# Eight stick-breaking heads, their filler slots in two orders, in a two-layer decoder trunk on one core

## What is computed

```python
def stick_breaking(q, k, v):                      # 8 heads
    z = einsum('bqhd,bkhd->bhqk', q_blk, k) * scale
    log_1m = where(causal, log_sigmoid(-z), 0.0)
    suffix = cumsum(log_1m, axis=3, reverse=True)
    att = where(causal, exp(log_sigmoid(z) + excl), 0.0)   # excl: suffix, shifted by one
    return einsum('bhqk,bkhd->bqhd', att, v)

def sb_dilated_mixer(h, w_in, rel_bias, w_out):
    proj = h @ w_in                               # 1024 x 3840
    qc, kc, vc, qd, kd, vd = split_cols(proj, CD_SPLITS)   # 3 x 512, 3 x 768
    oc = stick_breaking(heads(qc), heads(kc), heads(vc))
    od = dilated_mixture(heads(qd), heads(kd), heads(vd), rel_bias)
    return concatenate([oc, od], axis=-1) @ w_out
```

## Time and profile before

| | us |
|---|---|
| median of 3 runs | 1489.6 |
| lowest and highest | 1487.02, 1493.04 |
| the profiled execution's own time | 1487.59 |
| its span, first to last instruction | 1485.8 |

### The profile page before, as it was taken

One profiled execution on the slowest core, in us unless ns is written; L12 is line 12 of the kernel. 1 busy time (PEld: TensorE's weight loads), 2 busy tenths in 40 slices (PEclk: granted clock), 3 DMA queues, 4 the chain that ended last, 5 costly groups with the idle time before them and its releaser, 6 DMA issues.

```text
span 1485.8 us, 17068 instructions
## 1 busy us (share of the span) xinstructions
PE 1366.9 (92%) x6510; PEld 1123.3 (76%) x6510; DVE 622.7 (42%) x830; ACT 449.3 (30%) x603; POOL 506.8 (34%) x209
## 2 busy tenths in 40 slices
PE   3799998798999999999899999887889999999995
PEld 3678776588888888888788778656779888887884
DVE  5569751858643433400882232226486111010007
ACT  2343233314233223212323323333233323322121
POOL 2334331024345344444243333100125444444440
PEclk9899998799999999999999999997999999999998
DMA  9493632042556546643235322001113232234311
GB/s 335 134 97 102 212 117 82 22 176 72 181 175 209 197 152 232 182 126 100 104 116 180 109 85 72 29 1 57 36 50 100 99 99 99 92 79 154 99 57 56
DMA packets 93456, 173.79 MB, mean 117 GB/s; under 512 B 15655, under 2 KB 61879, under 8 KB 93276
## 3 DMA queue, kind: packets, MB, share of 16 engines
q1 hardware_dynamic: 90264, 169.63, 36.8%
q10 hardware_dynamic: 3140, 3.43, 0.9%
HBM read 170.87 MB, written 4.52 MB: 118 GB/s over the span
## 4 chain that ended last, share of the span: by engine, by line
PE 64%; issue 22%; DVE 6%; POOL 6%; ACT 2%; POOLq 0%; DVEq 0%; ACTq 0%
PE ps L1018 12%; PE ps L1020 12%; PE ps L1019 12%; PE ps L1050 6%; PE ps L1051 6%; PE ps L1052 6%; POOL w_lo L670 6%; PE ps L1462 1%; PE ps L1143 1%; PE ps L1145 1%; PE ps L1144 1%; PE ps L1434 1%; PE ps L1445 1%; PE ps L1448 1%; DVE rec L2101 1%
## 5 line engine op out<-in xcount | busy, mean ns | idle before, releaser
L670 POOL TENSOR_TENSOR w_lo<-raw,w_hi 128x1024 fp32r<-128x1024 f32 x205 | 506.6, 2474 | 943.8 <-ACT w_hi L690 943.4
L1018 PE MATMUL ps<-h_lo,w_hi 128*128 128x512 f32 (+2 forms) x1064 | 401.6, 377 | 13.6 <-DVE tmp L1867 6.2
L1019 PE MATMUL ps<-h_hi,w_hi 128*128 128x512 f32 (+2 forms) x1064 | 398.0, 374 | 0.0
L1020 PE MATMUL ps<-h_hi,w_lo 128*128 128x512 f32 (+2 forms) x1064 | 397.4, 374 | 0.0
L690 ACT ACTIVATE w_hi<-raw 128x1024 fp32r<-128x1024 f32 x205 | 216.0, 1056 | 487.8 <-PE ps L1052 189.0
L1018 PEld LDWEIGHTS ps<-h_lo,w_hi 128*128 128x128 f32 (+1 forms) x1064 | 204.1, 192 | 54.4 <-DVE tmp L1867 7.5
L1020 PEld LDWEIGHTS ps<-h_hi,w_lo 128*128 128x128 f32 (+1 forms) x1064 | 203.9, 192 | 35.1
L1019 PEld LDWEIGHTS ps<-h_hi,w_hi 128*128 128x128 f32 (+1 forms) x1064 | 203.9, 192 | 34.0
L1951 DVE TENSOR_TENSOR tmp<-tmp,ps 128x512 f32<-128x512 f32 x44 | 30.1, 688 | 264.2 <-PE ps L1020 264.2
L1050 PE MATMUL ps<-w_hi,hid_lo 128*128 128x512 f32 x352 | 137.9, 392 | 1.8 <-issue 0.9
L1052 PE MATMUL ps<-w_lo,hid_hi 128*128 128x512 f32 x352 | 137.5, 390 | 0.0
(11 more groups left out here) (228 smaller groups left out, 1491.5 us busy)
## 6 DMA issues: line engine op xcount, KB each, us to landing
raw<-wstream SPq DMA_DIRECT2D x205, 512.0 KB, 4.1
ada_raw<-astream SPq DMA_DIRECT2D x80, 512.0 KB, 4.6
ada_first<-astream SPq DMA_DIRECT2D x12, 512.0 KB, 10.0
ln_rows<-row_scratch SPq DMA_DIRECT2D x3, 1024.0 KB, 6.8
skew_scratch<-f_scratch ACTq DMA_DIRECT2D x1, 2304.0 KB
ada_first<-astream SPq DMA_DIRECT2D x8, 256.0 KB, 4.6
xa<-xT SPq DMA_DIRECT2D x4, 512.0 KB, 9.4
out<-xa SPq DMA_DIRECT2D x4, 512.0 KB, 3.5
```

Source lines behind the costliest of these rows:

```text
L670: nc.gpsimd.tensor_tensor(w_lo[:, slot, :], raw[:, slot % RAW, :], w_hi[:, slot, :].bitcast(F32), ALU.subtract).then_inc(sem("w_lo_ready"), 1)
L1018: pe.matmul(o, w_h, x_l, start=start, stop=False)
L1019: pe.matmul(o, w_h, x_h, start=False, stop=False)
L1020: return pe.matmul(o, w_l, x_h, start=False, stop=stop)
```

## The change

The list `FILL` gets a new order, q and k panels by turns and `vd1` ahead of `vd0`, and its slots now enter the weight stream in that order. Each entry goes with one head, on all engines: filler, tri of head h, av of head h - 1, z of head h + 1. The head loop without filler is gone. `vd0` is cut: its slots 0 and 1 stand ahead of tri of head 7, slot 2 ahead of av of head 7, slot 3 after the first four score rounds of the dilated part. z has one place in PSUM for all heads, banks 4 to 6, so z of head h + 1 waits for the exponential of head h; av has bank 7 throughout, and `stage` copies it after each second head, chunks 0 and 1 to `ada_acc`, 2 and 3 to `tmp`. Their high and low parts come later: ScalarE makes the high parts after the copies of `vd0`, VectorE the low parts after the row maxima. The score rounds use banks 4 to 7. The three DMAs of the bias (`load_bias`) are issued by ScalarE after the second entry, as before, which now belongs to head 1.

The core of the diff (the first list, ScalarE, TensorE, VectorE):

```diff
+FILL = ("qd0", "kd0", "qd1", "kd1", "qd2", "kd2", "vd1", "vd0")
+MIXED = [n for n in STAGES if n not in FILL]
+MIXED[MIXED.index("out10"):MIXED.index("out10")] = FILL
...
         use(name, free0, last(name), own=2)
@@ -355,15 +360,12 @@
         layer = norm // 2
...
@@ -407,15 +409,12 @@
     O_BANK = (4, 5, 6, 4)
     KV_BANK = (4, 5, 4, 5, 6, 7, 6)
     NG_BANK = (3, 6)
-    AV_BANK = (7, 7, 7, 3)
-
-    def sb_col(h):
-
-
-        return 0 if h > 4 and h % 2 else 4 * S
-
-
...
 
 
...
-            nc.scalar.activation(sb_a[h % 2][:], psf[:, sb_col(h):sb_col(h) + SC], ACT.Exp).then_inc(sem("att_exp"), 1)
+            nc.scalar.activation(sb_a[h % 2][:], psf[:, SB_COL:SB_COL + SC], ACT.Exp).then_inc(sem("att_exp"), 1)
 
         nc.scalar.preload_act_table_set("natural_log_exp_and_others")
         sb_first(0)
-        for i, part in enumerate(FILL):
-            if part[0] == "v":
+        for h, part in enumerate(FILL):
+            if part == "vd0":
+                hi_until(SLOTS[part][0] + 2 + RING)
+            elif part[0] == "v":
                 ahead(part)
                 v_blocks(part, v_dst[part])
             else:
                 qk_panel(part)
-            if i == 1:
+            if h == 1:
                 act.wait_ge(sem("skewed"), 16)
                 act.wait_ge(sem("ada_step"), 12 * KC)
                 load_bias(act)
-            if i % 2 == 0:
-                sb_second(i // 2)
-            else:
-                sb_first(i // 2 + 1)
-        hi_of_chunk(H_BASE["cat1"], 0)
-        for h in range(4, 8):
+            sb_second(h)
             if h + 1 < 8:
                 sb_first(h + 1)
-            sb_second(h)
-            if h % 2 == 0:
-                hi_of_chunk(H_BASE["cat1"] + h // 2 - 1, h // 2 - 1)
-        hi_of_chunk(H_BASE["cat1"] + 3, 3)
+        hi_until(SLOTS["vd0"][0] + 4 + 2)
+        v_blocks("vd0", v_dst["vd0"])
+        for n in range(4):
+            e = H_BASE["cat1"] + n
+            act.wait_ge(sem("h_tmp_ready"), e + 1)
+            nc.scalar.activation(h_hi[:, n, :], staged(n), ACT.Copy).then_inc(sem("h_hi_ready"), 1)
...
+            if only is None or 0 in only:
+                wait_pair(pe, name)
+            for i in range(count) if only is None else only:
...
             if h == 0:
                 pe.wait_ge(sem("f_ready"), 1)
-            elif h <= 4:
+            else:
                 pe.wait_ge(sem("att_exp"), h)
-            elif h >= 6:
-                pe.wait_ge(sem("att_exp"), h - 1)
...
-            if h == 2:
-                pe.wait_ge(sem("staged"), 1)
-            if h == 4:
-                pe.wait_ge(sem("h_tmp_ready"), H_BASE["cat1"] + 2)
+            if h in (2, 4, 6):
+                pe.wait_ge(sem("h_tmp_ready"), H_BASE["cat1"] + h // 2)
...
         sb_z(0)
-        for i, part in enumerate(FILL):
-            if part[0] == "v":
-                group(part, 2 if part == "vd0" else 4, S if part == "vd0" else 256)
+        for h, part in enumerate(FILL):
+            if part == "vd0":
+                group(part, 2, S, only=(0, 1))
+            elif part == "vd1":
+                group(part, 4, 256)
             else:
                 panel(part, KC, h_hi, h_lo)
-            if i % 2 == 0:
-                sb_tri(i // 2)
-            elif i < 7:
-                sb_av(i // 2)
-                sb_z(i // 2 + 1)
-        sb_z(4)
-        wait_free(pe, "vd1")
-        wait_free(pe, "vd1+")
-        for h in range(4, 8):
+            sb_tri(h)
+            if h:
+                sb_av(h - 1)
             if h + 1 < 8:
                 sb_z(h + 1)
-            sb_av(h - 1)
-            sb_tri(h)
+        group("vd0", 2, S, only=(2,))
         sb_av(7)
 
 
...
+            if score_bank(s) == AV_BANK:
+                pe.wait_ge(sem("h_tmp_ready"), H_BASE["cat1"] + 4)
...
+
+        for s in range(4):
+            scores(s)
+        group("vd0", 2, S, only=(3,))
+        for s in range(4, 16):
+            scores(s)
...
-        pe.wait_ge(sem("h_tmp_ready"), H_BASE["cat1"] + 4)
+        wait_free(pe, "vd0")
+        wait_free(pe, "vd0+")
...
+        def stage(n):
+
             dve.wait_ge(sem("av_done"), 2 * n + 2)
-            tmp_free(e)
-            src = ada_acc[:, 0:S] if n == 0 else ps[:, AV_BANK[n], :]
-            V.tensor_copy(tmp[:, e % 2, :], src).then_inc(sem("h_tmp_ready"), 1)
-            lo_of_chunk(e, n)
+            V.tensor_copy(staged(n), ps[:, AV_BANK, :]).then_inc(sem("h_tmp_ready"), 1)
+
+        def lo_of_staged(n):
+
+            dve.wait_ge(sem("h_hi_ready"), H_BASE["cat1"] + n + 1)
+            V.tensor_tensor(h_lo[:, n, :], staged(n), h_hi[:, n, :].bitcast(F32), ALU.subtract).then_inc(sem("h_ready"), 1)
...
         softplus(0)
-        for i, part in enumerate(FILL):
-            if part[0] == "v":
+        for h, part in enumerate(FILL):
+            if part == "vd1":
                 v_blocks(part)
-            else:
+            elif part != "vd0":
                 qk_panel(part)
-            if i % 2 == 0:
-                att_mask(i // 2)
-            else:
-                if i == 3:
-
-                    dve.wait_ge(sem("av_done"), 2)
-                    V.tensor_copy(ada_acc[:, 0:S], ps[:, AV_BANK[0], :]).then_inc(sem("staged"), 1)
-                softplus(i // 2 + 1)
-        dve.wait_ge(sem("staged"), 1)
-        sb_chunk(0)
-        for h in range(4, 8):
+            att_mask(h)
+            if h in (2, 4, 6):
+                stage(h // 2 - 1)
             if h + 1 < 8:
                 softplus(h + 1)
-            att_mask(h)
-            if h % 2 == 0:
-                sb_chunk(h // 2 - 1)
-        sb_chunk(3)
+        stage(3)
...
+        v_blocks("vd0")
...
+        for n in range(4):
+            lo_of_staged(n)
```

More of the change, by code:

```diff
@@ L95 @@
 OUT_K = {"out0": KC, "down0": FC, "out1": 6, "down1": FC}
+FILL = ("qd0", "kd0", "qd1", "kd1", "qd2", "kd2", "vd1", "vd0")
+MIXED = [n for n in STAGES if n not in FILL]
+MIXED[MIXED.index("out10"):MIXED.index("out10")] = FILL
 def slot_table():
     table, n = {}, len(FIRST)
-    for name in STAGES:
+    for name in MIXED:
         if name in ("va", "qa"):
@@ L333, in last @@
         return first + n - 1
-    V_FREE = {"va": 0, "vb": 1, "vc": 2, "vd0": 3, "vd1": 4}
+    V_FREE = {"va": 0, "vb": 1, "vc": 2, "vd1": 3, "vd0": 4}
     def group(name, free0, free1):
@@ L357, in build_program @@
             if layer == 1:
[L358 to L363, removed]
+                for e, name in enumerate(("qc0", "qc1", "kc0", "kc1") + FILL[:6]):
+                    use(name, [("qk1_act", e + 1), ("qk1_dve", e + 1)], last(name))
+                    if name == "kc1":
                         vgroup("vc")
+                vgroup("vd1")
                 vgroup("vd0")
-                vgroup("vd1")
         else:
@@ L409, in build_program, with staged @@
     NG_BANK = (3, 6)
-    AV_BANK = (7, 7, 7, 3)
-    def sb_col(h):
-        return 0 if h > 4 and h % 2 else 4 * S
-    FILL = [f"qd{p}" for p in range(3)] + [f"kd{p}" for p in range(3)] + ["vd0", "vd1"]
+    AV_BANK = 7
+    SB_COL = 4 * S
+    def staged(n):
+        return ada_acc[:, n * S:(n + 1) * S] if n < 2 else tmp[:, n % 2, :]
     v_dst = {
@@ L450, in score_bank @@
         h, part = score_step(s)
-        return (0, 1, 2, 4)[2 * (part % 2) + h % 2]
+        return 4 + 2 * (part % 2) + h % 2
     def part_tiles(part):
@@ L944, in sb_first @@
         def sb_first(h):
-            z = psf[:, sb_col(h):sb_col(h) + SC]
+            z = psf[:, SB_COL:SB_COL + SC]
             a = sb_a[h % 2]
@@ L1124, in panel, with group @@
                 m.then_inc(sem("slot_done"), 1)
-        def group(name, kk_n, width, beside=None):
+        def group(name, kk_n, width, beside=None, only=None):
             first, count = SLOTS[name]
-            wait_pair(pe, name)
-            for i in range(count):
+            if only is None or 0 in only:
+                wait_pair(pe, name)
+            for i in range(count) if only is None else only:
                 s = first + i
@@ L1425, in sb_z @@
             c, r = h // 2, 64 * (h % 2)
-            base = sb_col(h)
+            base = SB_COL
             if h == 0:
                 pe.wait_ge(sem("f_ready"), 1)
-            elif h <= 4:
+            else:
                 pe.wait_ge(sem("att_exp"), h)
-            elif h >= 6:
-                pe.wait_ge(sem("att_exp"), h - 1)
             for j in (0, 1, 2, 3):
@@ L1456, in sb_av @@
                 pe.wait_ge(sem("mod_ready"), 12)
-            if h == 2:
-                pe.wait_ge(sem("staged"), 1)
-            if h == 4:
-                pe.wait_ge(sem("h_tmp_ready"), H_BASE["cat1"] + 2)
+            if h in (2, 4, 6):
+                pe.wait_ge(sem("h_tmp_ready"), H_BASE["cat1"] + h // 2)
             for j in range(TB):
-                m = pe.matmul(ps[r:r + 64, AV_BANK[c], j * P:S], vc[:, j, h * 64:h * 64 + 64], sb_a[h % 2][:, OFS[j]:OFS[j] + WID[j]],
```

(26 more changed lines are left out.)

2 lines of the change are left out of this document (removed).

## The result

The changed kernel takes 1473.01 us (median of 4, 1472.21 to 1473.63) against 1491.14 for the kernel before on the same chip (median of 4, 1487.02 to 1493.04). The ratio is 0.9898, with a 95% interval of 0.9877 to 0.9918. A second comparison gave 1472.89 against 1487.49, ratio 0.9899, 0.9882 to 0.9916.

What follows compares the result with a forecast made beforehand. TensorE, busy 92% of the span, was taken as the bound, through its stops and lower clock. Gains of 18.1 and 1.4 us less 3.0 make 16.5, taken as 16.4: 1473.2 us against 1489.6, range 1468.5 to 1480.

Steps and rivals of the forecast that it cites:

- The walk through the heads: TensorE's queue through the heads, added from start to start: dilated scores begin at 980.79 for 998.86, gain 18.1 us.
- the unit lengths: Start-to-start lengths on TensorE in the heads: panel 11.06 us, tri 4.25, av plus z 4.64, vd1 11.69, vd0 slot 5.70.
- The new stop: TensorE behind head 0's tri: z of head 1 waits for head 0's exponential, one stop of 1.3 us.
- Nothing on the other engines is later than its panel: Heads: each chain from z through ScalarE and VectorE to tri, 10.1 us, ends within its 11.06 us panel.
- the slack of 0.85 us: Heads: time to spare between the masks' end at 887.58 and tri's start at 888.43.
- Rival A: Heads 4 to 7: masks beside GpSimd's splits cost 3.93 us more each; 15.7 us go back, 1488.9 us; chance 4%.
- Low parts off the path: VectorE ahead of the first dilated add: av's end to add takes 1.31 us for 2.69, gain 1.4 us.
- The hole among the scores: Dilated scores: the last vd0 slot on TensorE leaves VectorE dry before the fifth score, loss 3.0 us.
- The cover behind the maxima: VectorE behind the row maxima: four low parts, 2.8 us, fit in its 3.86 us wait for the first transposed tile.
- rival B: TensorE's clock drops once or twice more, behind head 0's stop or in the scores: 1475 to 1480 us; chance 18%.
- the sum: Whole kernel: gains of 18.1 and 1.4 less a loss of 3.0 make 16.5 us less, taken as 16.4.
- rival F: Better than forecast: TensorE's clock granted better where the output projection begins, 2 to 4 us more, 1469 to 1471; chance 8%.

Runs made afterwards that it cites:

- softplus_twice: The changed kernel with the softplus of every head done twice on VectorE; 1471.56 us, ratio 0.9900 to the kernel before.
- softplus_five_times: The changed kernel with the softplus of every head done five times on VectorE; 1482.96 us, ratio 0.9972 to the kernel before.
- the quarters: The changed kernel with the fourth slot of vd0 cut in four token blocks, one behind each four score rounds; 1467.76 us, ratio 0.9870 to the kernel before.
- packed: The changed kernel with its spread alone undone: heads 0 to 3 take two filler entries each, heads 4 to 7 none; 1504.99 us, ratio 1.0127.
- last_slot_in_head7: The changed kernel with the fourth slot of vd0 put back from among the dilated scores to head 7; 1477.95 us, again 1477.81.

## Why the prediction was right

It said 1473.2 us, and 1473.0 was measured; the ratio times its 1489.6 is 1474.4. Point by point:

- *The walk through the heads.* It forecast 832.17 for z of head 1 and 980.79 for the scores, counted from a trace in which z of head 0 began at 809.77. After began it 1.41 us later: z of head 1 at 833.58, as forecast (832.17 + 1.41); the scores at 983.53, where 982.20 would be the forecast. The heads took 172.35 us for 189.09 before, a gain of 16.7 for 18.1 forecast.
- *The 1.3 us that are missing there* are the step's one mis-sized term, the unit lengths. Tri was taken as 4.25 us, from a tri with a panel behind it. With an av behind it, the start of the next row comes 4.42 us later (927.29 to 931.71). A single slot of `vd0` was taken as a quarter of four, 5.70 us; between other steps it takes 5.96 (975.28 to 981.24). The length of a step, read from start to start, includes how the next kind of step is taken up. By parts: seven tri with an av behind them cost 1.2 us more than counted, the third slot of `vd0` 0.3 and the first two 0.1 (957.04 to 968.55), and the panels, 11.01 and 11.61 us for 11.06 and 11.69, gave back 0.3.
- *The new stop* behind head 0 was forecast at 1.3 us and is 1.33.
- *Nothing on the other engines is later than its panel.* Right, TensorE did not wait once. But the slack of 0.85 us was the wrong reading of the row behind it. It is the distance from the end of the masks, which follows the end of GpSimd's splits, to the end of the panel; VectorE's own chain could grow by 1.5 us for nothing (softplus_twice) and by 6.1 us for a stop of 1.26 (softplus_five_times). Rival A's condition came true and its price did not: the masks of heads 4 to 7 now run beside the splits and take 4.7 us, and all of it is hidden under the panels. Its 15.7 us took 4.69 us as work of VectorE where most of it was a wait. The Trainium skill's rule that was weighed ("SBUF — State Buffer", section Terms: one instruction holds the shared port pair to its end and the other engine is blocked) agrees for the masks, which read two operands from SBUF. The softplus reads one from PSUM and one from SBUF, and in softplus_five_times its five take 7.59 us beside the splits, 1.52 each for 1.49 alone, and the splits 4.77: neither held the other, so the rule as that section has it does not reach this instruction.
- *Low parts off the path*, 1.4 us: av's end to the first add is 1.30 us, for 2.69 before. Right.
- *The hole among the scores*, 3.0 us: measured 3.69. TensorE resumed the scores 8.74 us behind their start (983.53 to 992.27) for 8.45 counted, which is the longer slot, and the fifth add came 1.2 us behind that, for 0.75. That it is this slot, and only it, is shown by the quarters.
- *The cover behind the maxima* (3.86 us for 2.8) held: the first copy of a turned tile came 4.05 us behind the negated maxima both times (1028.82 after 1024.77, 1015.90 after 1011.85).
- *The clock in the heads* (rival B) did not fall in either profile of the changed kernel. It could have: behind the same stop of 1.33 us it fell in packed and in last_slot_in_head7, for about 1.6 us each time.
- *What the sum left out*: the rest of the dilated part took 36.2 us for 37.3, and the output projection to the end 427.7 for 428.2. The sum had nothing there; rival F had it, better granted clock, with 8% and 2 to 4 us. The rows bear F out in part, for 1.7 us. From the first transpose of a tile (L1522, now L1520) to the start of its fifth row in the timeline there are 7.66 us before and 6.51 after, at a granted clock of 0.62 and 0.74; from there to the output projection 23.09 and 23.11. The first 20 us of the output projection have 0.86 before and 0.89 after. The two windows, before and after, with the columns as above:

```profile
1026.85:1034.51 7.66, 7.66 (x45) 7.66 (x46) 1.38 (x2) 6.30 (x16) 0.00 (x0) 0.62 0.00 0
1013.92:1020.43 6.51, 6.50 (x44) 6.51 (x45) 1.91 (x3) 6.31 (x16) 0.00 (x0) 0.74 0.00 0
```

The work is the same in both, and length times clock is nearly so, 4.7 and 4.8. How long the clock stays low there differs from profile to profile, even between two of the same program (35.9 and 36.9 us with the last slot in head 7). What sets it was not isolated, so whether the change brought these 1.7 us or only met them is open.

The profiled execution took 1473.04 us for 1471.2 forecast. The 1.8 us are 1.4 ahead of the heads, where the programs are the same, 1.3 in the heads, 0.8 in the scores (23.86 for 23.1) and 1.7 less behind them. So two errors of 2.1 us together in heads and scores met a gain of 1.7 us from the clock that the sum didn't have, and that the median was met within 0.2 us is luck to that extent. Besides, the kernel before had a median of 1491.14 in this comparison, 1.5 us above the one that the forecast started from.

## What to carry to other kernels

Work that needs nothing of a chain is worth most when each link of the chain has a piece, and a piece is long enough when it is just longer than the chain: 11.06 us over 10.1 here. The same work in one lump, behind an engine that feeds another, starves it (5.99 us of TensorE cost VectorE 3.69 us, four pieces of 1.7 cost nothing). Before reading a slack from the distance of two rows, ask whether the late row is work or a wait: an operation that is 4.7 us long in one place and 0.76 in another holds a wait.

## What the runs showed of the hardware

The masks' time was not additive: 4.7 us for two beside the splits, 3.16 us when they began 1.5 us later, 0.76 behind them. TensorE's clock fell to 1.2 GHz behind each of four stops of 6.25 us in packed, where stops of 2.34 and 1.33 us had gone before a fall in the kernel before; after the change, with one stop of 1.33 us in 151.5 us, it stayed at 2.4 GHz. The same single stop of 1.33 us was followed by a fall in packed (0.50 from 844 to 846 us) and in one of the two profiles with the last slot in head 7 (0.50 from 839.10 to 842.25), and by none in the other eight profiles that have it. In softplus_five_times eight stops, of 1.33 us and less, some 20 us apart, left it at 1.00 from 835 to 995 us. So at this size the length of a stop alone doesn't tell whether the clock falls.
